# Key products shared three to one between VectorE and GpSimd, with the memory scan moved and the weights fetched in half tiles

## The reference

```
h = rms_norm(x)
zb, zc, zx, q, k, v, mq, gates = split(h @ w_in)      # 1024 columns each, gates 3 x 2048
Y_A = (zb * conv3(zc * zx)) @ w_conv_out
Y_B = differential_attention(q, k, v) @ w_diff_out    # sample rows: over 16 cached pages of 128 keys each
Y_C = memory_attention(mq, mk, mv) @ w_cross_out      # prompt rows: mk, mv = split(rms_norm(mem) @ w_mem_kv)
                                                      # sample rows: over 256 cached memory keys each
x = x + (sum_b sigmoid(gates_b) * Y_b) @ w_o
x = x + PEER(rms_norm(x))                             # top-16 of 16384 experts, 8 heads
```

## Time and profile before

| | us |
|---|---|
| median of 3 runs (2749.42 to 2750.76) | 2750.61 |
| the profiled execution | 2749.54 |
| its span, first to last instruction | 2747.8 |
| PE busy | 2443.3 (89%) |
| DVE busy | 1431.9 (52%) |
| POOL busy | 1055.8 (38%) |
| ACT busy | 352.9 (13%) |

### The profile page before, as it was taken

How to read it: one execution, slowest core, us unless ns; L and a number is a source line. 1 busy time by engine, 2 the same in 40 slices (tenths; PEclk the granted TensorE clock), 3 DMA queues, 4 the chain that set the end, 5 groups by cost and what they waited for, 6 DMA issues and landing times.

```text
span 2747.8 us, 27652 instructions
## 1 busy us (share of the span) xinstructions
PE 2443.3 (89%) x9109; PEld 1570.1 (57%) x9109; DVE 1431.9 (52%) x2306; ACT 352.9 (13%) x781; POOL 1055.8 (38%) x953
## 2 busy tenths in 40 slices
PE   9999998899999999999997777777999597777777
PEld 7888887778766678888884233332434142332333
DVE  3465566972322323002378877884554556554543
ACT  2111000012222211001112101111011011111110
POOL 1265566110222200000056555754544464445542
PEclk9999999999999999999999999998999899999999
DMA  7698999593799965447498999999999999999998
GB/s 225 225 343 311 323 345 333 203 343 123 280 353 352 355 215 187 159 149 235 138 369 344 422 418 417 416 418 422 422 413 422 412 408 418 419 421 418 416 421 370
DMA packets 305904, 919.33 MB, mean 335 GB/s; under 512 B 15738, under 2 KB 196050, under 8 KB 236756
## 3 DMA queue, kind: packets, MB, share of 16 engines
q0 software_dynamic: 122448, 725.64, 65.7%
q1 hardware_dynamic: 183332, 192.20, 21.4%
HBM read 909.08 MB, written 8.72 MB: 334 GB/s over the span
## 4 chain that ended last, share of the span: by engine, by line
PE 36%; DMA 24%; issue 13%; POOL 13%; DVE 11%; POOLq 2%; ACT 0%; DVEq 0%; SPq 0%; ACTq 0%
DMA sb_bregion<-in_peer_u_dram,sb_ring 14%; PE ps L788 13%; PE ps L800 6%; PE ps L694 4%; PE ps L1037 4%; DMA sb_mkv<-in_peer_u_dram,sb_ring 4%; DVE sb_bregion L1988 3%; POOL sb_ring L450 3%; POOL sb_mkv L450 3%; PE ps L888 2%; DMA sb_S<-in_peer_u_dram,sb_ring 2%; PE ps L778 2%; POOLq L441 2%; POOL sb_bregion L566 2%; POOL sb_wring L566 2%
## 5 line engine op out<-in xcount | busy, mean ns | idle before, releaser
L1037 PE MATMUL ps<-sb_wring,sb_ring 128*128 128x512 f32 x992 | 455.1, 608 | 86.7 <-DMA sb_wring<-in_peer_v_dram,sb_ring 86.6
L694 PE MATMUL ps<-sb_hT,sb_wring 128*128 128x264 f32 x1792 | 407.7, 388 | 3.4 <-DMA sb_wring<-in_w_in_dram 1.9
L1988 DVE CUSTOM_DVE_ANT_0 sb_bregion<-sb_bregion,sb_rows 128x2048 f32<-128x2048 f32 x128 | 293.5, 2293 | 217.2 <-DMA sb_bregion<-in_peer_u_dram,sb_ring 209.9
L1037 PEld LDWEIGHTS ps<-sb_wring,sb_ring 128*128 128x128 f32 x992 | 186.2, 194 | 354.4 <-issue 271.2
L694 PEld LDWEIGHTS ps<-sb_hT,sb_wring 128*128 128x128 f32 x1792 | 339.6, 191 | 62.2 <-issue 3.3
L788 PE MATMUL ps<-sb_hT,sb_wring 128*128 128x264 f32 x1536 | 368.2, 391 | 6.6 <-DMA sb_wring<-in_w_in_dram 5.1
L788 PEld LDWEIGHTS ps<-sb_hT,sb_wring 128*128 128x128 f32 x1536 | 289.2, 191 | 70.5 <-issue 16.4
L1037 PE MATMUL ps<-sb_oreg,sb_ring 128*128 128x512 f32 x496 | 236.1, 626 | 74.4 <-DMA sb_oreg<-in_peer_v_dram,sb_ring 52.0
L1037 PE MATMUL ps<-sb_hT,sb_ring 128*128 128x512 f32 x496 | 231.6, 614 | 53.6 <-DMA sb_hT<-in_peer_v_dram,sb_ring 47.5
L566 POOL DMA_INDIRECT sb_bregion<-in_peer_u_dram,sb_ring x132 | 185.7, 1407 | 226.1 <-DVEq L1376 194.5
L1037 PEld LDWEIGHTS ps<-sb_oreg,sb_ring 128*128 128x128 f32 x496 | 96.1, 200 | 213.5 <-issue 144.9
(11 more groups left out here) (376 smaller groups left out, 2785.1 us busy)
## 6 DMA issues: line engine op xcount, KB each, us to landing
sb_wring<-in_w_in_dram SPq DMA_DIRECT2D x52, 2048.0 KB, 13.0
sb_ring<-in_cache_k_dram POOLq DMA_DIRECT2D x64, 512.0 KB, 6.8
sb_mkv<-in_cache_k_dram POOLq DMA_DIRECT2D x64, 512.0 KB, 6.7
sb_mkv<-in_cache_v_dram POOLq DMA_DIRECT2D x48, 512.0 KB, 7.1
sb_rows<-in_cache_v_dram POOLq DMA_DIRECT2D x47, 512.0 KB, 7.2
sb_wring<-in_w_mem_kv_dram SPq DMA_DIRECT2D x8, 2048.0 KB, 11.7
sb_wring<-in_w_o_dram SPq DMA_DIRECT2D x8, 2048.0 KB, 8.1
sb_S<-in_cache_v_dram POOLq DMA_DIRECT2D x22, 512.0 KB, 6.8
```

What stands on the lines that cost most here:

```text
L694: last = mm(ps[:, (2 * r + c) % 4, 0:NT], wring[:, r, k, c * P:(c + 1) * P], rhs[:, k, :], start=(k == 0), stop=(k == KC - 1))
L1037: last = mm(ps[:, 4 * t + q, :], diag[:, k % 4, :], e_slots[v % ER][:, q * 512:(q + 1) * 512], start=False, stop=q_stop, skip_group_check= ...
L1988: st(V.tensor_tensor_reduce(out=u_slots[n % UR], in0=u_slots[n % UR], in1=h2, scale=1.0, scalar=0.0, op0=ALU.mult, op1=ALU.add, accum_out= ...
```

## The change

1. Key scan: POOL makes one product in four (page 3), DVE three (pages 0, 1 and 2) and all four sums. The three products share two buffers.
2. The memory scan moves forward on DVE, from behind `memory_key_norm` to right behind `row_norms`, in front of the conv steps. It uses the eight slots of the key scan. ACT waits for its end (`token_done` 2 + 16) before the first memory chunk goes into `mkv`. POOL loads the memory pages of tokens 0 and 1 at the end of the key scan.
3. A weight slot holds 1024 of the 2048 rows of 512 columns, in row pieces of 2 KB. PE adds up the first half of the rows for four chunks in four banks, then the second half. The slot is fetched again after its four half chunks. The memory stage makes 8 chunks of 512 columns in place of 16 of 256, in the four banks. The first gate block is fetched when the last first half of the memory weights is used.
4. The last two of the 16 column groups of x are turned behind the first half chunk.

The diff, cut to its core:

```
@@ SP
-            stream(16, w_in, 3 * DC, C_QKV, None)
-            stream(12, w_in, 0, C_CONV, ("chunk_full", C_CONV))
-            stream(8, w_mem, 0, C_MEM, ("chunk_full", C_MEM))
+            def fetch_half(h, src, col):
+                sp.dma_start(whalf[:, h], src[:, h * BC:(h + 1) * BC, ds(col, 2 * BLK)]).then_inc(w_landed[h], 16)
+
+            def stream_halves(n, src, col, h0, c0, chunks):
...
+                with sp.Fori(0, n - 1) as i:
+                    sp.wait_ge(s["half_full"], i + (h0 + 1))
+                    fetch_half(0, src, i * (2 * BLK) + (col + 2 * BLK))
+                    sp.wait_ge(s["chunk_full"], i * chunks + (c0 + chunks))
+                    fetch_half(1, src, i * (2 * BLK) + (col + 2 * BLK))
+
+            stream_halves(8, w_in, 3 * DC, 0, C_QKV, 4)
+            stream_halves(6, w_in, 0, H_CONV, C_CONV, 4)
+            stream_halves(4, w_mem, 0, H_MEM, C_MEM, 2)
@@ SP, first gate block
-                    sp.wait_ge(s["chunk_full"], C_O - 2)
+                    sp.wait_ge(s["half_full"], H_GATE)
@@ POOL
-                for r in (1, 3):
-                    pool.wait_ge(k_landed[4 * half + r], i * 64 + 16 * (g // 2 + 1))
-                    st(nc.gpsimd.tensor_tensor(kpages[4 * half + r], kpages[4 * half + r], qb[:, par, :], ALU.mult))
-                    pool.sem_inc(s["kprod_ready"], 1)
+                pool.wait_ge(k_landed[4 * half + 3], i * 64 + 16 * (g // 2 + 1))
+                st(nc.gpsimd.tensor_tensor(kpages[4 * half + 3], kpages[4 * half + 3], qb[:, par, :], ALU.mult))
+                pool.sem_inc(s["kprod_ready"], 1)
...
+            pool.wait_ge(s["kpage_used"], 8 + TS * PAGES)
+            load_memory(0)
+            load_memory(1)
             pool.wait_ge(s["q_ready"], 2)
             pool.dma_start(mq_dram, rows[0:TS, 2, 3 * DC:4 * DC]).then_inc(s["q_scratch"], 16)
             pool.wait_ge(s["q_scratch"], 32)
...
+            load_query(0)
+            load_query(1)
+            load_memory(2)
+            load_memory(3)
...
             for b in range(2, TS):
                 pool.wait_ge(s["token_done"], 2 + TS + (b - 2) + 1)
                 load_query(b)
+                if b + 2 < TS:
+                    load_memory(b + 2)
@@ PE, linear
+                    pe.wait_ge(w_landed[0], i * 16 + 16 * pair)
+                    for c in range(4):
+                        pe.wait_ge(s["chunk_taken"], i * 4 + (n0 + c + 1))
...
+                        last = half_chunk(0, c, rhs, fresh and first and c == 0)
+                        if c == 3:
+                            last.then_inc(s["half_full"], 1)
...
+                    pe.wait_ge(w_landed[1], i * 16 + 16 * pair)
+                    for c in range(4):
+                        half_chunk(1, c, rhs, fresh and first and c == 0).then_inc(s["chunk_full"], 1)
@@ PE, memory stage
+            with pe.Fori(0, 2) as i:
+                for g in range(2):
+                    for h in range(2):
+                        pe.wait_ge(w_landed[h], i * 32 + 16 * (G_MEM // NR + g + 1))
+                        for t in range(2):
+                            if h == 0:
+                                pe.wait_ge(s["chunk_taken"], i * 4 + (C_MEM + 2 * g + t + 1))
+                            for k in range(h * BC, (h + 1) * BC):
+                                last = mm(ps[:, 2 * g + t, :], memT[:, k, t * P:(t + 1) * P], whalf[:, h, k % BC, :], start=(k == 0), stop=(k == KC - 1))
@@ ACT
-            act.wait_ge(s["token_done"], 2 + TS)
+            act.wait_ge(s["token_done"], 2 + 2 * TS)
@@ DVE, score_group
+                for r in range(3):
+                    dve.wait_ge(k_landed[4 * half + r], landed)
+                    if r == 2:
+                        st.reach(k0 + 3)
+                    elif g:
+                        st.reach(k0)
+                    st.run(TT(prods[r % 2], slots[r], qb[:, par, :], ALU.mult))
+                    for p in ((), (0, 1), (2,))[r]:
+                        st.reach(k0 + (1, 2, 5)[p])
+                        signal("kpage_used")
+                        st.run(RED(out(p), by_head(prods[p % 2]), X, ALU.add))
+                dve.wait_ge(s["kprod_ready"], i * 8 + (g + 1))
                 st(RED(out(3), by_head(slots[3]), X, ALU.add))
                 signal("kpage_used")
```

More of the change, by code:

```diff
@@ L122, in build @@
         cflat = conv[:, :, :].rearrange("p a b -> p (a b)")
+        whalf = wring[:, :, :, :].rearrange("p r (k two) n -> p r k (two n)", two=2)
         x_rows, h2_rows = rows[:, :, 0:D], rows[:, :, D:2 * D]
@@ L130, in build @@
         ring_flat = ring4[:, :, :].rearrange("p a b -> p (a b)")
-        conv_y = conv[:, 2 * BC:3 * BC, :].rearrange("p a b -> p (a b)")
-        mem_pages = [ring4[:, n, :] for n in range(4)] + [conv_y[:, n * DC:(n + 1) * DC] for n in range(2)]
-        MEM_PAIR = [0, 1, 2, 0, 1, 2, 1, 2]
+        MEM_PAIR = [2, 3, 0, 1] * 2
         scores = cflat[:, 0:3 * 2 * PH * NKEY].rearrange("p (t n) -> p t n", t=3)
@@ L656, in _, with turn_columns @@
                 turn_x(2, k).then_inc(s["xT_full"], 1)
-            for k in range(7, KC):
+            def turn_columns(k):
                 pe.wait_ge(s["xT_taken"], k - 6 if k < 14 else k - 2)
@@ L661, in _, with turn_last_columns @@
                 turn_x(2, k).then_inc(s["xT_full"], 1)
+            def turn_last_columns():
+                turn_columns(14)
+                turn_columns(15)
+            for k in range(7, 14):
+                turn_columns(k)
                 if k == 7:
@@ L684, in turn_memory, with chunk @@
                 transpose_rows(h2_rows, k, 6 + k % 2, TILES[0:2]).then_inc(s["xT_full"], 1)
-            def chunk(r, c, n, rhs, fresh=False):
+            def chunk(r, c, n, rhs):
                 pe.wait_ge(s["chunk_taken"], n + 1)
-                if fresh:
-                    pe.wait_ge(s["xT_taken"], 11)
                 for k in range(KC):
+                    last = mm(ps[:, (2 * r + c) % 4, 0:NT], wring[:, r, k, c * P:(c + 1) * P], rhs[:, k, :], start=(k == 0), stop=(k == KC - 1))
+                last.then_inc(s["chunk_full"], 1)
@@ L697, in linear @@
             def linear(g0, n_blocks, c0, rhs, turn=None, pending=None, fresh=False, aside=None):
                 def four(i, pair, n0, first):
-                    for r in range(NR):
-                        pe.wait_ge(w_landed[r], i * 16 + 16 * pair)
-                        for c in range(2):
-                            q = 2 * r + c
-                            chunk(r, c, i * (2 * NR) + (n0 + q), rhs, fresh and first and q == 0)
-                            if aside:
-                                aside(n0 - c0 + q)
-                            if first and q == 0:
-                                if pending:
-                                    pending()
-                            elif turn:
-                                turn((q - 1) % 4, i * (2 * NR) + (n0 - c0 + q - 1))
+                    pe.wait_ge(w_landed[0], i * 16 + 16 * pair)
@@ new lines, in four @@
+                    for c in range(4):
+                        pe.wait_ge(s["chunk_taken"], i * 4 + (n0 + c + 1))
+                        if fresh and first:
+                            pe.wait_ge(s["xT_taken"], 8 + c)
+                        last = half_chunk(0, c, rhs, fresh and first and c == 0)
+                        if c == 3:
+                            last.then_inc(s["half_full"], 1)
+                        if c == 0:
+                            if first and pending:
+                                pending()
+                            elif turn and not first:
+                                turn(3, i * 4 + (n0 - c0 - 1))
@@ L1522, in _, with score_memory @@
             signal("q_ready")
+            def score_memory(b):
+                par, k0 = b % 2, st.k
+                dve.wait_ge(qb_landed[par], 64 + 16 * (b // 2 + 1))
+                for t in range(2):
+                    n = 2 * MEM_PAIR[b] + t
+                    dve.wait_ge(k_landed[n], 256 + 16 * (MEM_PAIR[:b].count(MEM_PAIR[b]) + 1))
+                    st.run(TT(prods[t], kpages[n], qb[:, par, :], ALU.mult))
+                for t in range(2):
+                    st.reach(k0 + t + 1)
+                    st.run(RED(Sm_f[:, b * 8 + t * 4:b * 8 + t * 4 + 4], prods[t].rearrange("p (g w) -> p g w", w=MD), X, ALU.add))
+                st.settle()
+                signal("token_done")
+            for b in range(TS):
+                score_memory(b)
             dve.wait_ge(s["chunk_taken"], C_MEM + 4)
```

137 lines of the change are left out of this document (48 added, 89 removed).

## The result

| | before | after |
|---|---|---|
| median of 8 runs each, us | 2750.02 | 2758.77 (2755.07 to 2760.58) |
| ratio, 95% interval | | 1.003 (1.0021 to 1.004) |
| span of the profiled execution, us | 2747.8 | 2754.3 |

The change makes the kernel slower by 0.3%, 8.7 us. The forecast was 15.7 us faster. It was wrong in sign, and the time lies just above its range. The shape of the forecast came true all the same: the key scan ends 47 us earlier, PE has one wait on ACT in the memory stage, about as long as forecast (12.1 us against 11.5), and none before the gate stage. But both sides of that wait, the memory scan's end and PE's arrival, are 24 us late; that its length came out right is luck.

What follows compares the result with a forecast made beforehand. PE bounds the kernel, held up by the POOL-bound key scan. Scan end 424 puts the gate stage at 569 against 584.6, gaining 15.7 us: 2749.5 - 15.7 = 2733.8, median 1.1 higher, so 2735; range 2720 to 2757.

Steps and rivals of the forecast that it cites:

- The gate start follows through one to one: From the gate stage on PE is busy, so a gain at its start counts one to one to the end.
- From 116: Key scan's start, taken from the kernel before: 116 us.
- Key scan 308 us: Length of the key scan: 296 us plus 12 for late pages, from 116 to 424 us.
- Groups without collisions: Key scan: 32 groups at 8.4 us each, DVE and POOL in step.
- Collisions 8: Key scan: 7 query loads push POOL's product into DVE's third, 1.2 us each, 8 us in all.
- Loop turns 19.4: Key scan: POOL's loop turns stay, 2 x 8.3 + 2.8 = 19.4 us.
- Late pages 12: Key scan: pages landing later beside the weights, charged 12 us (bounds 0 and 30).
- E to PE's restart, 86 us: Norms, query store and load, memory scan of 42 us, ACT's first copy: PE restarts 86 us after the key scan's end.
- E: Time at which the key scan ends: 424 us, bounds 412 and 450.
- PE at the fifth chunk at 498.5: Memory stage: PE reaches its wait on ACT at 498.5 us, conv end 443.5 plus 55 for four chunks.
- weights come late: Rival: more page traffic delays weights, 1 us for each of 20 blocks; 8.5 come through, 2743 us; chance 0.07.
- Rows of 2 KB: Weight fetches: larger rows would get a larger part beside the pages if engines take turns by packet; no size given.

Runs made afterwards that it cites:

- b_halves: Kernel before with half weight tiles, late column groups (parts 3 and 4) and the early root alone; 2741.24 us, ratio 0.9971.
- a_root: Changed kernel with ACT's root of the query norms moved in front of its wait for chunk 8; 2746.25 us, ratio 0.9987.
- a_stores: Changed kernel with the stores of new keys and values issued behind the memory scan's loads; 2753.87 us, ratio 1.0017.
- d_halfpages: Changed kernel with the early root, loading only the first 512 of each key page's 1024 columns; 2724.36 us in one run.
- f_unsplit: Changed kernel with the early root and products two and two again (parts 2, 3 and 4); 2804.43 us in one run.
- c_both: Changed kernel with both the early root and the late stores of keys and values; 2739.8 us, ratio 0.9965.
- b_split: Kernel before with the three to one product split (part 1) only, and the 60-column root one conv step earlier; 2777.03 us, ratio 1.0097.
- e_rows2k: Changed kernel with the early root and key pages asked for in 2 KB row pieces, which did not take; 2746.2 us, ratio 0.9985.
- c_noscan: Changed kernel with the early root and the memory scan back behind `memory_key_norm` (parts 1, 3 and 4); 2741.31 us, ratio 0.9968.

## Why the prediction was wrong

**What went wrong, in short.** The change's time is set by ACT's chain: the scan's start, the scan, and the way behind it. It is 24.6 us longer than forecast, 11.1 of it at the start (127.2 for 116), 3.8 in the scan and 9.7 behind it, and that turns 15.7 us faster into 8.9 slower. The late weights are a second error of the same size, which the change's own time does not show.

**The gate start follows through one to one:** right, within the noise of single executions. 8.9 us late at the gate stage, 8.7 at `w_o` and in the medians. Not so in b_halves, where what had covered DVE's work was gone, as the prediction said of that case.

**"From 116":** this is the first failed step, and the largest for the time. The scan's start was taken over from before as if nothing of the change stood ahead of it. I had followed what half tiles do to SP and PE, and not what four chunks that end close together do to the instructions queued behind a chunk on ACT. It moved the scan's start by 10.9 us against before; taken out in a_root, it gives back 12.4 us at the gate stage and 12.5 of time.

**Key scan 308 us:** 311.8 measured, by terms that cancel. Groups without collisions, 8.4 us each, 268.8: they took 278.1 (small idle pieces between a product and its sum, 7.8 us in 32 places, and ahead of the next group, 10.8 in 31, were half left out). Collisions 8: 20.2; in step the engines do not mesh for nothing in every group, and late in the scan every second pair of products meets POOL's. Loop turns 19.4: 13.5. Late pages 12: DVE waits for no page but the first, so nothing as a wait; with half pages the collisions fall by 7 us. That the sum came out near is luck. The Trainium skill's "SBUF — State Buffer", section "Who interferes with whom", says that a product with two inputs in SBUF contends with GpSimd and a reduce does not; the trace agrees (4.52 us for two products, sums at 1.21), and how often they meet had to be measured.

**E to PE's restart, 86 us:** 96 measured. Norms and the query's way were right within 0.6 us (first memory product at E + 42.7, forecast 43.2, though the store came back faster and the load landed slower). The memory scan was 52.4, not 42: I counted its busy part, 39, and 3 us more, while DVE's waits for queries came to 15.3 us, 8.45 of them for the third, behind 2 MB of stores. a_stores takes 7.6 of the 10 us off.

**PE at the fifth chunk at 498.5:** 522.9 measured, the largest miss of a single time. It adds nothing to the change's own time, since PE still waits 12.1 us there for ACT; it is the bound that comes next. The conv branch ends 15.0 us later than forecast (13.3 of waits, the rest half clock); b_halves has 0.3 of such waits, d_halfpages 0.4, so these come from the faster page traffic. In the memory stage come 6.0 of wait and 3.3 of half clock. These are another matter: before had two waits of 3.1 us for memory weights, the forecast put them at nothing without giving a reason, and about 6 us of them stand in b_halves, f_unsplit and d_halfpages as well, where the page traffic is less. As a whole this is the rival "weights come late", to which I gave 0.07; its 20 us were right for PE (24), and so was its rule that only what exceeds the wait on ACT comes through. a_root shows it alone: gate start 3.5 us before that of before, time 3.3 us less, where the rival said 7. The step that failed: I had a landing of 13.5 us, a limit of 14.3 and 20% more pages beside it, and called that "may miss". A DMA share of 0.94 before left no room; the same estimate that put the pages' need at 95% of what they could get should have stretched the weights too. The kernel before was within 0.8 us of this loss.

**The two losses overlap.** Chain and PE are each some 24 us late, and the gate stage follows the one that comes later. The chain does; PE's 24.4 us alone, less the 11.5 us it had in hand, would have made the gate stage 12.9 late, near 582, and a_root, whose chain is early enough, starts it at 581.1. That is why a_root stops at 3.3 us under before. c_both reaches 10.2 us, with shorter waits for weights in the profile.

**Rows of 2 KB:** the prediction left open whether larger weight rows get a larger part beside the pages. At equal page traffic the landing falls from 18.4 to 15.2 us. The Trainium skill's "DMA: Bandwidth & Descriptors", section "Queues, rings and completion order", has each DMA engine take turns between its queues by packet, and says that such a packet holds several descriptors. The profile counts one packet for each row piece of the weights (2.0 KB each here, 1.0 KB in b_split), so the shorter landing fits the page only if its packets grow with the pieces, which no run here shows. Since e_rows2k did not change the pages' packets, fewer packets as such remain as a rival.

**What would have been the better forecast:** part 3 alone moves ACT's due time to half of the stage, 498.5 by the prediction and 494 in b_halves, behind the end of the slow scan, 485.8. By the prediction's own numbers (without the late root, which it did not see) the wait on the scan was gone without parts 1 and 2, and these had no wait left to shorten. b_halves and c_noscan are level, and both are 17 us faster than the change.

**Left open:** why POOL stands still at both loop turns in eleven kernels and at none with half pages; what makes PE wait for memory weights; whether weights land sooner with 2 KB rows by their share or by the number of packets; and how c_both's 10.2 us come about in its other executions, which spread over 2733.9 to 2743.3 us with one at 2756.

## What to carry to other kernels

When chunks are regrouped so that several end together, go through every engine's program for what is queued behind the first of them: here one small root behind one copy moved the whole scan by 11 us. Here, in a stage that ran at a DMA share of 0.94, the faster reader was paid for by the stream beside it, and the transfer to price is the one whose landing is nearest to its limit (13.5 of 14.3 us). And take the parts of a change in turn against the wait that they are to remove: if a cheap part removes it alone, as in b_halves, the dear parts have nothing left to gain.

## What was unexpected of the hardware

- A stream of 2 MB transfers through SP's queue lands in 14.0 us with rows of 1 KB and in 11.6 with rows of 2 KB beside the same pages; beside a faster page stream, 18.4 and 15.2. Total traffic with 2 KB rows reaches 366 GB/s at a share of 0.97 in the change.
- Splitting a contiguous row of 4 KB into two pieces in the description of a load left the number of packets as it was (17266).
- DVE's product and POOL's, both with two inputs in SBUF, take turns so strictly that two products of DVE need 4.5 to 5.0 us with one of POOL's between, beside 2.36 alone.
- At a loop turn POOL stands still for 8.8 to 12.5 us, at both turns in eleven kernels (8.84 and 9.37 us in b_halves, 12.45 and 10.67 in b_split), and with half pages at none. With one product less in the loop's body it is no shorter (11.5 us in the change, 9.44 in the earlier trace rows).
